# Forming the low part of the weights on GpSimd instead of VectorE in the projection stages

## The chip, the cores and the metric

The kernel runs on one core of a Trainium2 chip. A core has five engines: TensorE (PE in the profile, its weight loads PEld), VectorE (DVE), ScalarE (ACT), GpSimd (POOL) and SyncE (SP), which issues the DMAs. They run side by side and wait for each other by semaphores. The metric is the device time of one execution in microseconds; less is better.

## The reference, cut to what matters

The reference is a network of two parts in float32: two layers that mix attention, a gated recurrence, a short convolution and a Fourier branch, and then a block with latent attention, a state space scan and a feed-forward part. There are 256 context and 1024 latent positions of width 1024. What the change touches is the large projections from the normalized activations:

```python
lat = split_cols((rms_norm(h, norm_g) * (1.0 + scale) + shift) @ w_in)     # 1024 -> 3584, per layer
cx = split_cols((rms_norm(hc, norm_g) * (1.0 + scale_c) + shift_c) @ w_in)
```

and the input projection of the second block, in the same form.

## The kernel before, in words

The products need more precision than one pass of TensorE on rounded operands gives. So each operand is split in two: a high part, which is the operand rounded to the type fp32r, and a low part, which is the rest. A product is the sum of three matmuls: high by high, high by low, low by high.

`project_split` (line 358) does this for the projections. It is called nine times: three times in each of the two layers (queries, keys, values and the convolution's inputs; the Fourier branch; the recurrence's gates) and three times in the second block (latents; z; the state convolution's inputs). A call is one stage: a block of code in which each engine has its own loop over the same list of steps, with a barrier behind it. There are 384 steps in all. A step is one slice of 128 rows of the contraction (`kk`), with all the tokens and columns that are summed at that time in PSUM banks. In step i

- ScalarE (lines 465 to 478) waits until TensorE has finished step i-2, because there are NX = 2 buffers for the activations, and casts them to `x_high` (line 469). Then it casts the step's weights to `w_high` (line 473; NW = 3 buffers). Then it empties PSUM banks of a finished group, if there are any, and does a piece of work of a helper.
- VectorE (lines 497 to 511) waits for `x_high` and subtracts it from the activations, which gives `x_low` (line 500). It waits for `w_high` and subtracts it from the weights, which gives `w_low` (line 504). Then it empties banks and does its piece of the helper's work.
- TensorE (lines 515 to 536) waits for `x_low` and `w_low` and issues three matmuls for each group of the step (lines 526, 527, 528).

A helper (`beside=`) is work of another kind that is dealt out over the steps: `Heads` normalizes and rotates queries and keys, `ConvBranch` is the short convolution, `Gates` computes the recurrence's gates, `Decays` those of the state space scan, and `StateConv` (line 219) is a convolution of five taps, whose products stand at line 321. The order of everything on an engine is that of the code; nothing is planned by costs.

A step's shape is given by the width of the activations and the number of weight columns. The names in the trace are those of the tiles: `buf_a` holds the activations, `w` the weights as they came from memory, `ps` is PSUM. GpSimd has no part in these stages. Elsewhere it does sums of the softmax, parts of the recurrence (lines 862, 863) and some subtractions of the same kind as `x_low` and `w_low` (lines 3275, 3650). Line 2140 is VectorE's `x_low` in the feed-forward part, which has its own code, and line 2061 is GpSimd's product there.

Of the kernel before, what the change touches and what calls it, by code (L numbers as in the profile page):

```python
# [8 lines left out]
F32 = mybir.dt.float32  # L9
# [348 lines left out]
def project_split(k, jobs, *rooms, moves=(), beside=None, banks=8):  # L358
# [8 lines left out]
    NX, NW = 2, 3  # L367
    passes, groups, steps = [], [], []
# [37 lines left out]
    def place(name, shape):  # L406
        for room in rooms:
            if room.o + int(np.prod(shape[1:])) * 4 <= room.end:
                return room(name, shape, F32R)
        assert False, name  # L410
    xh, xl = ([place(f"x_{p}{i}", [P, width]) for i in range(NX)] for p in ("high", "low"))
    widest = max(j["cols"] for j in jobs)
    wh, wl = ([place(f"w_{p}{i}", [P, widest]) for i in range(NW)] for p in ("high", "low"))
    evac_act, evac_dve, x_high, x_low, w_high, w_low, moved, silued = sems = k.sems(
        "evacuated_by_act", "evacuated_by_dve", "x_high", "x_low", "w_high", "w_low", "moved", "silu_in_bank")
# [4 lines left out]
    def x_of(s):  # L420
        return s["job"]["x"](s["kk"], s["t0"], s["tn"])

    def w_of(s):
        return ws.tile(s["chunk"])[:, s["kk"] % KD, :]

    def evacuations(i, by):

        return [g for g in steps[i - 1]["groups"] if g["by"] == by or by == "act" and g["do"] == "times_silu"
                ] if i and steps[i - 1]["last"] else []
# [8 lines left out]
    with nc.Block() as block:  # L438
        @block.sync
        def _(sp):  # L440
            for dst, src in moves:
                sp.dma_start(dst, src).then_inc(moved, 16)
            if beside:
                beside.load(sp)
            ws.load_until(sp, ws.taken)
            if moves:
                sp.wait_ge(moved, 16 * len(moves))

        @block.scalar
        def _(act):  # L450
            def evacuate(gs):
                for i, g in enumerate(gs):
                    if i == 0 and "free" in g["job"]:
                        g["job"]["free"](act)
                    act.wait_ge(ws.products, g["ready"])
                    if g["do"] == "times_silu":
                        act.activation(g["out"], g["out"], ACT.Silu).then_inc(silued, 1)
                        continue
                    func = ACT.Silu if g["do"] == "silu" else ACT.Copy
                    dst, out = g["job"]["dst"](g["sub"], g["n"]), g["out"]  # L460
                    if len(dst.shape) == 3:
                        out = out.rearrange("p (t x) -> p t x", x=P)
                    act.activation(dst, out, func).then_inc(evac_act, 1)

            parts = beside.act(act, landed) if beside else iter(())
            for i, s in enumerate(steps):
                if i >= NX:
                    act.wait_ge(ws.products, steps[i - NX]["after"])
                act.copy(xh[i % NX][:, 0:s["tn"]], x_of(s)).then_inc(x_high, 1)  # L469
                ws.wait(act, s["chunk"])  # L470
                if i >= NW:
                    act.wait_ge(ws.products, steps[i - NW]["after"])
                act.copy(wh[i % NW][:, 0:s["job"]["cols"]], w_of(s)).then_inc(w_high, 1)
                evacuate(evacuations(i, "act"))
                if beside and i >= beside.first:
                    next(parts, None)
            evacuate(evacuations(len(steps), "act"))
            for _ in parts:
                pass

        @block.vector
        def _(dve):
            def evacuate(gs):
                for i, g in enumerate(gs):
                    if i == 0 and "free" in g["job"]:
                        g["job"]["free"](dve)
                    dve.wait_ge(ws.products, g["ready"])
                    dst = g["job"]["dst"](g["sub"], g["n"])
                    if g["onto"]:
                        if g["do"] == "times_silu":  # L490
                            dve.wait_ge(silued, g["silued"])
                        dve.wait_ge(done_of[g["onto"]["by"]], g["onto"]["count"])
                        dve.tensor_tensor(dst, g["out"], dst, ALU.mult).then_inc(evac_dve, 1)
                    else:
                        dve.tensor_copy(dst, g["out"]).then_inc(evac_dve, 1)

            parts = beside.dve(dve, landed) if beside else iter(())
            for i, s in enumerate(steps):
                dve.wait_ge(x_high, i + 1)
                dve.tensor_tensor(xl[i % NX][:, 0:s["tn"]], x_of(s), xh[i % NX][:, 0:s["tn"]].bitcast(F32),  # L500
                                  ALU.subtract).then_inc(x_low, 1)
                dve.wait_ge(w_high, i + 1)
                n = s["job"]["cols"]
                dve.tensor_tensor(wl[i % NW][:, 0:n], w_of(s), wh[i % NW][:, 0:n].bitcast(F32),  # L504
                                  ALU.subtract).then_inc(w_low, 1)
                evacuate(evacuations(i, "dve"))
                if beside and i >= beside.first:
                    next(parts, None)
            evacuate(evacuations(len(steps), "dve"))
            for _ in parts:  # L510
                pass

        @block.tensor
        def _(pe):
            parts = beside.pe(pe, landed) if beside else iter(())
            for i, s in enumerate(steps):
                pe.wait_ge(x_low, i + 1)
                pe.wait_ge(w_low, i + 1)
                for g in s["groups"]:
                    if s["kk"] == 0 and g["before"]:  # L520
                        pe.wait_ge(done_of[g["before"]["by"]], g["before"]["count"])
                    xs = [x[i % NX][:, g["a"]:g["a"] + g["tn"]] for x in (xh, xl)]
                    c = slice(g["sub"] * P, (g["sub"] + 1) * P) if s["fm"] else slice(0, s["job"]["cols"])
                    w = [v[i % NW][:, c] for v in (wh, wl)]
                    lhs, rhs = (w, xs) if s["fm"] else (xs, w)
                    pe.matmul(g["out"], lhs[0][:, :], rhs[0][:, :], start=(s["kk"] == 0), stop=False)  # L526
                    pe.matmul(g["out"], lhs[0][:, :], rhs[1][:, :], start=False, stop=False)  # L527
                    mm = pe.matmul(g["out"], lhs[1][:, :], rhs[0][:, :], start=False, stop=s["last"])  # L528
                    if s["last"]:
                        mm.then_inc(ws.products, 1)  # L530
                if not s["last"]:
                    mm.then_inc(ws.products, 1)
                if beside and i >= beside.first:
                    next(parts, None)
            for _ in parts:
                pass
# [635 lines left out]
def mixer_layer(k, layer, XT, YT):  # L1172
# [27 lines left out]
    def qkv(t, end=None):  # L1200
        r = rows[t // 5]
        return r[:, t % 5, :] if end is None else r[:, t % 5:t % 5 + end - t, :]

    heads = Heads(k, layer, qkv, qt, kt, v, spare(), KD + 1)
    project_split(k, [tm(HALF, lambda s, n: qkv(n), "copy", all_tiles),
                      fm(BR, lambda c: YT[:, 2 + c, :], "silu", ALL_BLOCKS),
                      dict(fm(HALF, lambda s: gate[:, s % 2, :], "copy", ALL_BLOCKS), second="times_silu",
# [3 lines left out]
    def unit(nk, *parts):  # L1211
# [13 lines left out]
    conv = ConvBranch(k, layer, u, gate, lay)  # L1225
    done_rows = d["branches"].rearrange("(c p) t -> p c t", p=P)
    project_split(k, [dict(fm(HALF, lambda s: fu[:, s, :] if s < 2 else YT[:, 4 + s, :], "copy", ALL_BLOCKS), silu_from=2)],
                  Layout(k, lay.o, A_C), moves=[(done_rows[:, 2:4, :], YT[:, 2:4, :])], beside=conv)
    lay = Layout(k, A_R + 2 * T * 4, A_C)
# [8 lines left out]
    rest = lay.o  # L1238
    gates = Gates(k, layer, a, key, lay, KD + 2)
    project_split(k, [fm(BR, lambda c: a[0][:, c, :], "copy", ALL_BLOCKS),  # L1240
                      fm(BR, lambda c: a[1][:, c, :], "copy", ALL_BLOCKS),
                      fm(BR, lambda c: YT[:, 4 + c, :], "silu", ALL_BLOCKS),
# [2918 lines left out]
```

## Time and profile before

| What | Value |
|---|---|
| median of 3 runs | 4411.45 us (4408.74 to 4412.24) |
| the profiled execution | 4406.21 us |
| its span | 4404.2 us |
| TensorE busy | 3866.2 us (88%) |
| TensorE's weight loads | 2991.1 us (68%) |
| VectorE busy | 2710.5 us (62%), 4101 instructions |
| ScalarE busy | 1995.1 us (45%) |
| GpSimd busy | 963.1 us (22%), 1100 instructions |

The span runs from the first to the last instruction of the profiled execution. Busy times are the union of an engine's records. Matmuls are pipelined, so that records of neighbours overlap, and 88% is not a measure of how near TensorE is to its peak. What is idle on an engine says something only if the work that ends last waits for it, so the rows further down are of single steps.

### The profile page before, as it was taken

The numbers are of one execution on the slowest core, as the hardware profiler recorded it, in microseconds if no ns is written. First come the engines' busy times: TensorE is split into PE (matmuls) and PEld (weight loads), VectorE is DVE, ScalarE is ACT, GpSimd is POOL, SyncE is SP. The second block draws the span as 40 slices with busy tenths as digits, with TensorE's granted clock in tenths as the row PEclk, the third lists the DMA queues.
The fourth block names the chain that finished last, engine by engine and source line by source line (L and its number), as shares of the span: only waits on it lengthen the run. The fifth ranks groups of instructions, "written<-read, shape, count | busy, mean of one in ns | idle before, by whom it ended". The sixth has DMA issues, their size and how long they took to land. (4 is left out here: it accounts for less than half of the span.)

```text
span 4404.2 us, 58870 instructions
## 1 busy us (share of the span) xinstructions
PE 3866.2 (88%) x22208; PEld 2991.1 (68%) x22208; DVE 2710.5 (62%) x4101; ACT 1995.1 (45%) x3667; POOL 963.1 (22%) x1100
## 2 busy tenths in 40 slices
PE   6988888987999787986789999799787979999898
PEld 5765777876775675765656666477655758888686
DVE  4756477966765567965555555447865655566555
ACT  4544265544544266434434444345543543343344
POOL 0016004610007002600055555400082000111000
PEclk7989999999999898998999999899898989999999
DMA  5100113654100111032000000212003541111243
GB/s 177 39 15 6 59 39 126 232 185 160 39 20 1 54 39 49 1 121 83 29 5 5 9 5 5 77 36 67 4 3 115 187 149 39 39 58 39 91 153 139
DMA packets 211274, 297.08 MB, mean 67 GB/s; under 512 B 74090, under 2 KB 139882, under 8 KB 210996
## 3 DMA queue, kind: packets, MB, share of 16 engines
q1 hardware_dynamic: 210436, 293.14, 20.1%
q8 instruction: 179, 2.93, 0.3%
q14 instruction: 99, 0.81, 0.1%
q0 software_dynamic: 416, 0.05, 0.0%
q10 hardware_dynamic: 144, 0.15, 0.0%
HBM read 262.17 MB, written 31.03 MB: 67 GB/s over the span
## 5 line engine op out<-in xcount | busy, mean ns | idle before, releaser
L500 DVE TENSOR_TENSOR x_low<-buf_a,x_high 128x1280 fp32r<-128x1280 f32 (+4 forms) x384 | 376.2, 980 | 430.7 <-ACT x_high L469 427.6
L526 PE MATMUL ps<-x_high,w_high 128*128 128x512 f32 (+1 forms) x1344 | 495.7, 369 | 102.8 <-DVE w_low L504 97.8
L469 ACT CAST x_high<-buf_a 128x1280 fp32r<-128x1280 f32 (+4 forms) x384 | 327.6, 853 | 560.6 <-PE ps L528 490.9
L527 PE MATMUL ps<-x_low,w_high 128*128 128x512 f32 (+1 forms) x1344 | 483.9, 360 | 0.0
L528 PE MATMUL ps<-x_high,w_low 128*128 128x512 f32 (+1 forms) x1344 | 482.9, 359 | 0.0
L2939 PE MATMUL ps<-w_high,x_high 128*128 128x512 f32 x896 | 364.6, 407 | 97.1 <-DVE w_low L2782 93.3
L526 PEld LDWEIGHTS ps<-x_high,w_high 128*128 128x128 f32 x1344 | 258.1, 192 | 174.7 <-DVE x_low L500 114.9
L2940 PE MATMUL ps<-w_low,x_high 128*128 128x512 f32 x896 | 358.7, 400 | 0.0
L2941 PE MATMUL ps<-w_high,x_low 128*128 128x512 f32 x896 | 358.5, 400 | 0.0
L2782 DVE TENSOR_TENSOR w_low<-w,w_high 128x1024 fp32r<-128x1024 f32 x170 | 208.0, 1223 | 197.8 <-ACT w_high L2895 197.7
L3469 DVE TENSOR_REDUCE mx<-ps 128x1 fp32r<-128x1280 f32 x128 | 190.7, 1491 | 199.8 <-PE ps L3344 199.3
L2895 ACT CAST w_high<-w 128x1024 fp32r<-128x1024 f32 x170 | 178.3, 1049 | 263.7 <-PE ps L2941 256.2
L2048 PE MATMUL ps<-x_high,w_high 128*128 128x512 f32 x704 | 278.1, 395 | 12.4 <-DVE w_low L2144 12.4
L528 PEld LDWEIGHTS ps<-x_high,w_low 128*128 128x128 f32 x1344 | 257.9, 192 | 38.5
L526 PE MATMUL ps<-w_high,x_high 128*128 128x512 f32 (+2 forms) x608 | 220.7, 363 | 70.1 <-DVE w_low L504 66.7
L527 PEld LDWEIGHTS ps<-x_low,w_high 128*128 128x128 f32 x1344 | 258.4, 192 | 32.6
L2050 PE MATMUL ps<-x_high,w_low 128*128 128x512 f32 x704 | 279.6, 397 | 0.0
L2049 PE MATMUL ps<-x_low,w_high 128*128 128x512 f32 x704 | 278.7, 396 | 0.0
L2939 PEld LDWEIGHTS ps<-w_high,x_high 128*128 128x128 f32 x896 | 173.6, 194 | 147.9 <-issue 111.7
L2140 DVE TENSOR_TENSOR x_low<-attn_t,x_high 128x512 fp32r<-128x512 f32 x176 | 145.5, 827 | 202.5 <-ACT x_high L2093 192.8
L2093 ACT CAST x_high<-attn_t 128x512 fp32r<-128x512 f32 x176 | 109.1, 620 | 299.2 <-PE ps L2050 297.6
L862 POOL TENSOR_TENSOR x<-a 128x128 f32<-128x128 f32 x252 | 115.9, 460 | 526.9 <-POOLq L73 421.3
(446 smaller groups left out, 8959.9 us busy)
## 6 DMA issues: line engine op xcount, KB each, us to landing
w<-in_w_out SPq DMA_DIRECT2D x26, 2048.0 KB, 8.6
w<-in_w_mod SPq DMA_DIRECT2D x24, 2048.0 KB, 9.3
w<-in_w_down SPq DMA_DIRECT2D x15, 2048.0 KB, 7.8
w<-in_w_in SPq DMA_DIRECT2D x26, 1024.0 KB, 5.2
w<-in_w_up SPq DMA_DIRECT2D x22, 1024.0 KB, 7.6
w<-in_w_in SPq DMA_DIRECT2D x7, 2048.0 KB, 9.6
x<-in_x SPq DMA_DIRECT2D x16, 512.0 KB, 8.8
scratch_branches<-buf_b SPq DMA_DIRECT2D x4, 1280.0 KB, 5.7
```

The source lines that it names most:

```text
L469: act.copy(xh[i % NX][:, 0:s["tn"]], x_of(s)).then_inc(x_high, 1)
L500: dve.tensor_tensor(xl[i % NX][:, 0:s["tn"]], x_of(s), xh[i % NX][:, 0:s["tn"]].bitcast(F32), ALU.subtract).then_inc(x_low, 1)
L526: pe.matmul(g["out"], lhs[0][:, :], rhs[0][:, :], start=(s["kk"] == 0), stop=False)
L527: pe.matmul(g["out"], lhs[0][:, :], rhs[1][:, :], start=False, stop=False)
L528: mm = pe.matmul(g["out"], lhs[1][:, :], rhs[0][:, :], start=False, stop=s["last"])
L2048: pe.matmul(o, wh[w % NW][:, c], xh[x % NX][:, :], start=(kk == 0), stop=False)
L2049: pe.matmul(o, wh[w % NW][:, c], xl[x % NX][:, :], start=False, stop=False)
L2050: mm = pe.matmul(o, wl[w % NW][:, c], xh[x % NX][:, :], start=False, stop=(kk == KD - 1))
L2782: dve.tensor_tensor(wl[i % NW][:, :], ws.tile(s["chunk"])[:, s["kk"] % PER, :], wh[i % NW][:, :].bitcast(F32), ALU.subtract).then_inc(w_lo ...
L2939: pe.matmul(o, a[:, t], wh[i % NW][:, c], start=(s["kk"] == 0), stop=False)
L2940: pe.matmul(o, a[:, t], wl[i % NW][:, c], start=False, stop=False)
L2941: mm = pe.matmul(o, b[:, t], wh[i % NW][:, c], start=False, stop=s["last"])
```

## The change

VectorE's loop in `project_split` loses the wait for `w_high` and the subtraction that forms `w_low`. A new loop of GpSimd, which had none in this function, does the same subtraction with the same operands: it waits for the step's `w_high` and for its own subtraction of the step before, and raises the same semaphore `w_low`, on which TensorE waits.

```diff
+        @block.gpsimd
+        def _(pool):
+            for i, s in enumerate(steps):
+                pool.wait_ge(w_high, i + 1)
+                if i >= 1:
+                    pool.wait_ge(w_low, i)
+                n = s["job"]["cols"]
+                pool.tensor_tensor(wl[i % NW][:, 0:n], w_of(s), wh[i % NW][:, 0:n].bitcast(F32),
+                                   ALU.subtract).then_inc(w_low, 1)
+
         @block.vector
...
                 dve.wait_ge(x_high, i + 1)
                 dve.tensor_tensor(xl[i % NX][:, 0:s["tn"]], x_of(s), xh[i % NX][:, 0:s["tn"]].bitcast(F32),
                                   ALU.subtract).then_inc(x_low, 1)
-                dve.wait_ge(w_high, i + 1)
-                n = s["job"]["cols"]
-                dve.tensor_tensor(wl[i % NW][:, 0:n], w_of(s), wh[i % NW][:, 0:n].bitcast(F32),
-                                  ALU.subtract).then_inc(w_low, 1)
                 evacuate(evacuations(i, "dve"))
```

VectorE's order in the stage with the state convolution, before; the numbers behind the names tell buffers apart:

```order
L500 TENSOR_TENSOR x_low_467_31649<-buf_a_53,x_high_465_31647 128x1280
L504 TENSOR_TENSOR w_low_472_31654<-w_2_50,w_high_469_31651 128x256
L321 SCALAR_TENSOR_TENSOR xbc_conv_461_31644<-xbc_raw_460_31643,taps_31646,xbc_conv_461_31644 128x255
L321 SCALAR_TENSOR_TENSOR xbc_conv_461_31644<-xbc_raw_460_31643,taps_31646,xbc_conv_461_31644 128x1023
L500 TENSOR_TENSOR x_low_468_31650<-buf_a_53,x_high_466_31648 128x1280
```

The same place on VectorE in the changed kernel, where line 510 is what was line 500:

```order
L510 TENSOR_TENSOR x_low_467_32001<-buf_a_53,x_high_465_31999 128x1280
L321 SCALAR_TENSOR_TENSOR xbc_conv_461_31996<-xbc_raw_460_31995,taps_31998,xbc_conv_461_31996 128x255
L321 SCALAR_TENSOR_TENSOR xbc_conv_461_31996<-xbc_raw_460_31995,taps_31998,xbc_conv_461_31996 128x1023
L510 TENSOR_TENSOR x_low_468_32002<-buf_a_53,x_high_466_32000 128x1280
L321 SCALAR_TENSOR_TENSOR xbc_conv_461_31996<-xbc_raw_460_31995,taps_31998,xbc_conv_461_31996 128x255
```

The convolution's products now stand right behind `x_low`. On GpSimd, the start of the changed program, up to the first subtractions of the first projection stage:

```order
L4155 MEMSET const-float32-0.0 128x1
L4155 MEMSET const-float32-1.0 128x1
L4155 MEMSET const-bfloat16-1.0 128x1
L4155 MEMSET const-uint8-127 128x1
L72 ISA x2
L481 UNCONDITIONAL_BRANCH
L488 ISA
L488 TENSOR_TENSOR w_low_55_725<-w_3_51,w_high_52_722 128x512
L488 TENSOR_TENSOR w_low_56_726<-w_3_51,w_high_53_723 128x512
L488 TENSOR_TENSOR w_low_57_727<-w_3_51,w_high_54_724 128x512
```

Before, the first arithmetic of GpSimd's program stood in the attention behind that stage (line 3641). Now 384 subtractions are spread over the nine stages, in the order of the steps.

## Rows read from the trace of the kernel before

**Rows 1.** The nine projection stages, sum over their windows: us busy by engine
```profile
sum 1351.00, PE 1204.53 PEld 1002.32 DVE 861.84 ACT 700.41 POOL 0.00; mean PE 133.84 PEld 111.37 DVE 95.76 ACT 77.82 POOL 0.00
```

**Rows 2.** Waits of TensorE: who waited for whom, us in total, times, longest
```profile
PEld ps L526 <- DVE x_low L500: 160.7, 88, 10.0
...
PE ps L526 <- DVE w_low L504: 164.5, 97, 30.8
```

**Rows 3.** VectorE's subtractions by form: count, us busy, mean ns, idle before, releaser
```profile
L500 DVE TENSOR_TENSOR x_low<-buf_a,x_high 128x1280 fp32r<-128x1280 f32 x128 | 190.9, 1491 | 130.3 <-ACT x_high L469 128.5
L504 DVE TENSOR_TENSOR w_low<-w,w_high 128x512 fp32r<-128x512 f32 x208 | 142.5, 685 | 24.5 <-ACT w_high L473 22.5
L500 DVE TENSOR_TENSOR x_low<-buf_a,x_high 128x640 fp32r<-128x640 f32 x96 | 79.1, 824 | 120.2 <-ACT x_high L469 119.4
L500 DVE TENSOR_TENSOR x_low<-buf_a,x_high 128x512 fp32r<-128x512 f32 x112 | 77.4, 691 | 136.3 <-ACT x_high L469 135.9
L504 DVE TENSOR_TENSOR w_low<-w,w_high 128x256 fp32r<-128x256 f32 x160 | 66.9, 418 | 0.0
```

**Rows 4.** Timeline, step of 512 columns, x 512: start and length in us
```profile
2934.49 0.69 DVE L500 TENSOR_TENSOR x_low<-buf_a,x_high 128x512 fp32r<-128x512 f32 x1 [1.43 <-ACT x_high L469]
2935.10 0.69 DVE L504 TENSOR_TENSOR w_low<-w,w_high 128x512 fp32r<-128x512 f32 x1
...
2936.35 0.39 PE L526 MATMUL ps<-w_high,x_high 128*128 128x512 f32 x1
```

**Rows 5.** Timeline, step of 256 columns, x 1280
```profile
566.94 0.40 ACT L473 CAST w_high<-w 128x256 fp32r<-128x256 f32 x1
...
567.07 1.49 DVE L500 TENSOR_TENSOR x_low<-buf_a,x_high 128x1280 fp32r<-128x1280 f32 x1 [1.67 <-ACT x_high L469]
568.48 0.42 DVE L504 TENSOR_TENSOR w_low<-w,w_high 128x256 fp32r<-128x256 f32 x1
...
569.07 0.32 PE L526 MATMUL ps<-x_high,w_high 128*128 128x256 f32 x1
```

**Rows 6.** Timeline, steps of 512 columns, x 256
```profile
242.51 0.61 ACT L473 CAST w_high<-w 128x512 fp32r<-128x512 f32 x1
...
242.57 0.36 PE L526 MATMUL ps<-x_high,w_high 128*128 128x256 f32 x1 [0.41 <-DVE w_low L504]
...
242.64 0.42 DVE L500 TENSOR_TENSOR x_low<-buf_a,x_high 128x256 fp32r<-128x256 f32 x1 [0.21 <-ACT x_high L469]
243.16 0.69 DVE L504 TENSOR_TENSOR w_low<-w,w_high 128x512 fp32r<-128x512 f32 x1
```

**Rows 7.** Timeline, step of 256 columns, x 640
```profile
688.66 0.42 DVE L504 TENSOR_TENSOR w_low<-w,w_high 128x256 fp32r<-128x256 f32 x1
...
689.22 0.36 PE L526 MATMUL ps<-w_high,x_high 128*128 128x256 f32 x1 [0.38 <-DVE w_low L504]
```

**Rows 8.** GpSimd's subtractions elsewhere, by form, columns as in rows 3
```profile
L3275 POOL TENSOR_TENSOR q_low<-q,q_high 128x512 fp32r<-128x512 f32 x16 | 20.6, 1285 | 1.3
...
L3650 POOL TENSOR_TENSOR q_low_row<-qt,q_high_twice 64x256 fp32r<-64x256 f32 x4 | 2.8, 722 | 0.2
```

**Rows 9.** Timeline of the feed-forward part, VectorE and GpSimd
```profile
3694.99 2.42 POOL L2061 TENSOR_TENSOR g_a<-g_a,act 128x1024 f32<-128x1024 f32 x1 [71.15 <-ACT act L2086]
...
3695.44 2.52 DVE L2140 TENSOR_TENSOR x_low<-attn_t,x_high 128x512 fp32r<-128x512 f32 x1 [1.38 <-ACT x_high L2093]
```

**Rows 10.** The recurrence: timeline, and line 863's ns least/median/most
```profile
709.40 0.64 DVE L945 TENSOR_TENSOR qe<-eq,qk 128x256 f32<-128x256 f32 x1
709.73 0.59 POOL L862 TENSOR_TENSOR x<-a 128x128 f32<-128x128 f32 x1
...
L863 POOL TENSOR_TENSOR x<-a x252: 392/574/669, 705.2 to 1873.5; 128x128 f32<-128x128 f32 x126
```

**Rows 11.** Timeline, a step of the gates' stage where VectorE is late
```profile
1612.22 0.40 ACT L473 CAST w_high<-w 128x256 fp32r<-128x256 f32 x1
...
1613.77 1.49 DVE L500 TENSOR_TENSOR x_low<-buf_a,x_high 128x1280 fp32r<-128x1280 f32 x1
```

## The prediction, made before the changed kernel was run

> **What bounds the kernel now.** I read the windows of the nine projection stages first: in their 1351 us TensorE has 1204.5 us of records, VectorE 861.8, and GpSimd none [rows 1]. So TensorE is near full there, and GpSimd has room in time. Then the table of waits, narrowed to TensorE: at the first matmul of a projection step its queue stands 164.5 us for VectorE's w_low and 160.7 us (by the weight load's record, partly the same time) for x_low [rows 2]. Then VectorE's instructions by form, which give the classes of the 384 steps: x_low 1280 wide in 128 steps, 640 in 96, 512 in 112, and by the code 256 in 32 and 768 in 16; w_low has 512 columns in 208 steps, 256 in 160, and 192 in the other 16 [rows 3]. Last, the timeline of one step of each class, for what is late in it.
>
> The question for a step is whether its operands are ready before TensorE has finished the step ahead. There are two x buffers, so ScalarE's cast for step i starts when step i-2 is done. From there runs a chain: x_high, x_low beside w_high, w_low, first matmul. If the chain is longer than one step of TensorE's, TensorE idles in every second step: two steps then take the chain plus one step of matmuls. So what the chain grows by, beyond its spare time, is paid once in two steps. TensorE starts 0.15 us after w_low's end at the earliest (688.66 + 0.42 = 689.08 against 689.22 [rows 7]), so spare time is what lies beyond 0.15.
>
> - 512 columns, x 512 wide: w_low ends at 2935.79 and TensorE takes the step at 2936.35 [rows 4], spare 0.41 us. The stretches with x 640 or 768 wide and 512 columns have a longer matmul part and spare over 0.8 us (my reading of their timelines; only that they have more than 0.55 matters).
> - 256 columns, x 1280 wide: w_low ends at 568.90, TensorE takes it at 569.07 [rows 5]: spare 0.02.
> - 512 columns, x 256 wide: TensorE already waits, 0.41 us at 242.57 for w_low [rows 6]. 256 columns, x 640 wide: it waits 0.38 us [rows 7]. Spare 0.
>
> **The change, part by part.** Removed from VectorE: 384 subtractions, 142.5 + 66.9 + some 5.6 us (16 of the 192 wide) = 215 us of records [rows 3]. That is a relief to an engine that has idle time in most steps, and worth something only where x_low itself starts late. Added to GpSimd: the same 384. Nothing else moves; the casts, the matmuls and the DMA queues keep their places, and GpSimd has no other work in these stages that could queue behind.
>
> Cost of one on GpSimd: the same operation, f32 minus f32 to fp32r, stands in the trace: 1.285 us for 512 columns, 0.722 us for 256 [rows 8]. VectorE takes 0.685 and 0.418 [rows 3]. For 192 columns I take 0.58, on the line through the two.
>
> The Trainium skill ("GPSIMD Engine Reference", Performance versus the Vector engine) gives 4497 ns for a tensor_tensor of 2048 columns on GpSimd, 2.2 ns a column. By that, as an estimate, 512 columns would take 1.12 us, the chain of the 512 by 512 steps would grow by 0.39 us, less than its spare, and the sum below would lose its largest class (13 us). The row for exactly this operation says 1.285, and I go by the row.
>
> When can it start? w_high ends 0.3 to 0.5 us after x_high, and VectorE is then in x_low, which reads two tensors of SBUF. The trace shows what such a pair does. VectorE's x_low of 512 columns takes 0.69 us alone [rows 3], but 2.52 us when it meets a GpSimd product that began at 3694.99 and ended at 3697.41: it ends 0.55 us after that one, so it did nothing until GpSimd had ended, but for some 0.14 us of start [rows 9]. The other way round, GpSimd's 128 column product behind VectorE's product of two SBUF tensors ends at 710.32, 0.28 us after VectorE's end at 710.04, and its record is 0.59 us against 0.39 at the least [rows 10]: it waited too, all but 0.11 us of its start. So the two run one after the other, and beside each other the change can't put them. In a steady step x_low has the way first.
>
> The growth of the chain then is, per class:
> - 512 columns, x 512 wide: x_low ends 2935.18; w_low on GpSimd ends at 2935.18 + 1.28 - 0.12 = 2936.34 instead of 2935.79, +0.55, less the spare 0.41 = 0.14. TensorE would now stand still in every second step, and a step that begins after a pause also pays some 0.1 for a pipeline that fills again (the first matmul's record is 0.36 us after a pause [rows 6, 7] and 0.32 without one, of the same 256 columns [rows 5]; 0.04 is the least, 0.1 my estimate). 56 pairs by 0.24 = 13.4 us.
> - 512 columns, x 256 wide: here x_low is over (243.06) before w_high (243.12), so nothing is in the way: 243.12 + 0.08 (the hand-off, an estimate) + 1.28 = 244.48 instead of 243.85 [rows 6], +0.63. 16 pairs: 10.1 us.
> - 256 columns, x 1280 wide: x_low ends 568.56; + 0.72 - 0.12 = 569.16 instead of 568.90, +0.26, less 0.02. 64 pairs by 0.24 = 15.4 us.
> - 256 columns, x 640 wide: +0.26, 16 pairs: 4.2 us. 192 columns: about +0.2, 8 pairs: 1.6 us.
> - x 640 or 768 wide with 512 columns, 64 steps: +0.55 is covered by the longer matmul part: 0.
> - The first step of a stage has no step ahead to hide in: six of 0.6 and three of 0.26 = 4.4 us.
> - Where VectorE is late, it gains. x_low starts at 1613.77 though x_high and w_high were done by 1612.62 [rows 11]; w_low would be formed before it, and 0.34 us of VectorE's queue goes. I count 18 such steps of 256 columns (8 have x 640 wide), nearly all in the gates' stages: -6.1. But there, and in the stage with the state convolution, GpSimd's w_low also holds up the two-tensor operations that VectorE works off beside, which gives a third back: -4 net.
>
> Sum: 13.4 + 10.1 + 15.4 + 4.2 + 1.6 + 4.4 - 4 = 45.1, say +45 us. The profiled execution took 4406.2 us (span 4404.2), 5 below the runs' median of 4411.45, so 4451 for it and 4456 on the median; I give 4454, that is 45 beyond 4409, between the two. Bounds: below, the chain grows by nothing in the 256 column classes (the case without a conflict, next part) and the filling costs nothing, +5. Above, w_low waits for one more VectorE operation in the stages with side work, +70.
>
> **Rivals.**
> 1. No conflict for the two engines: w_low begins 0.08 us after w_high. For 256 columns with x 1280 wide it ends at 567.34 + 0.80 = 568.14, before x_low (568.56), and VectorE's 0.34 us leave the chain: the step is then bound by TensorE, gain at most 0.02 in steady steps, and 0.34 in the late ones. For 512 columns nearly nothing changes, since there GpSimd hardly waits after w_high. Sum: 13.4 + 10.1 + 3.6 for the six beginnings - 6.1, less about 14 for VectorE's relief where x_low and the side work share the queue (40 steps by 0.34, an estimate), some +7: 4416. For it speaks that x_low is fully read by one engine; against it rows 9 and 10, both with f32 operands of this kind. 8%.
> 2. Faster: VectorE's queue decides. If the stages with side work (gates, state convolution, heads: some 200 steps) are held by VectorE's order, each of the 0.34 to 0.6 us taken from it counts wherever TensorE waits. Without a conflict the costs are 13.4 + 10.1 + 3.6 = 27, so it decides from 80 such steps by 0.34 on. With 110 of them, 25 steps of the 512 column classes by 0.6 beside: 27 - 37 - 15 = -25, 4384. Against it: VectorE idles 130.3 + 120.2 + 136.3 us before x_low for x_high [rows 3], so its queue is seldom what holds. 5%.
> 3. VectorE keeps the way: when x_low ends, the next operation that it has in line, a product or the state convolution's of 0.48 us, goes first, and w_low comes after it. Rows 10 speak against it (in that stretch the two alternate one by one), but there GpSimd had always been first in line. It costs one such operation, 0.3 to 1.4 us, in the 50 or so steps where a two-tensor operation stands right behind x_low and the chain is bare, mostly paid once in two steps: about +20 more, 4474. 15%.
>
> **How the numbers follow.** Forecast (one after the other, in turn) 70%, rival 1 8%, rival 2 5%, rival 3 15%; the rest, 2%, is left to something else on the faster side. Under the forecast 4454, with 4440 to 4468 from the uncertain filling (6 us) and the late steps (4 to 8 us). The range takes rival 3 in and reaches half way to rival 1: 4430 to 4480. A change under 0.2% (9 us) could not be told from none here: rival 1 lies on that edge, so faster 6%, same 8%, slower 86%.
>
> **What would show it.** After: GpSimd's w_low rows near 1.28 and 0.72 us when alone and longer where they begin inside x_low; w_low's end 0.55 (512 columns, x 512 wide) and 0.26 us (256) later against the step's x_high; PE's wait for w_low at a step's first matmul up from 164.5 us by some 40 us; new pauses in every second step of the 512 by 512 stretch near 2936, none where x is 640 wide with 512 columns. x_low should stay at 0.69 and 1.49 us in steady steps; if many of them are longer, GpSimd is first in line more often than I think. Wrong would make it: w_low rows of 256 columns that overlap x_low and still take 0.72 (rival 1), or that end only after the next VectorE operation (rival 3).

## The result, and the profile after

The changed kernel takes 4452.0 us (median of 4 runs, 4448.9 to 4452.6) against 4411.8 us before (4 runs, 4408.7 to 4413.7): a ratio of 1.0093, with a 95% interval of 1.0081 to 1.0106. It is slower by 40 us, forecast was 4454. Its profiled execution has a span of 4450.4 us, 46.2 more than before.

The sum of the windows of the nine projection stages, which answers to [rows 1], and the subtractions by form, which answer to [rows 3] (columns as there). The windows of before were cut in whole microseconds and are 9 us wider than the stages, so 1351 to 1382.5 isn't their growth: from first cast to last matmul the stages grew from 1341.8 to 1382.4, by 40.6 us.

```profile
sum 1382.50, PE 1216.80 PEld 997.54 DVE 789.64 ACT 698.51 POOL 547.62; mean PE 135.20 PEld 110.84 DVE 87.74 ACT 77.61 POOL 60.85
```

```profile
L488 POOL TENSOR_TENSOR w_low<-w,w_high 128x512 fp32r<-128x512 f32 x208 | 285.9, 1375 | 803.9 <-ACT w_high L473 802.0
L510 DVE TENSOR_TENSOR x_low<-buf_a,x_high 128x1280 fp32r<-128x1280 f32 x128 | 200.4, 1566 | 142.2 <-ACT x_high L469 140.6
L488 POOL TENSOR_TENSOR w_low<-w,w_high 128x256 fp32r<-128x256 f32 x160 | 246.0, 1538 | 447.0 <-ACT w_high L473 445.5
```

VectorE is busy 72 us less in the stages, although 215 us of subtractions left it. Part of the difference is overlap of neighbouring records, but most is waiting inside the records that stayed: added up one by one, x_low takes 29 us more than before and VectorE's other operations 84 us more. GpSimd has 548 us more: a subtraction of 256 columns has a record of 1.54 us on average, although one that runs alone takes 0.72 [rows 8], and longer than one of 512 columns. So half of such a record is waiting. x_low is longer too, 1.566 us against 1.491 [rows 3].

A steady step of 256 columns, x 1280 wide, in the timeline (start and length in us), which answers to [rows 5]:

```profile
578.00 0.40 ACT L473 CAST w_high<-w 128x256 fp32r<-128x256 f32 x1
...
578.12 1.49 DVE L510 TENSOR_TENSOR x_low<-buf_a,x_high 128x1280 fp32r<-128x1280 f32 x1 [2.33 <-ACT x_high L469]
...
578.47 1.75 POOL L488 TENSOR_TENSOR w_low<-w,w_high 128x256 fp32r<-128x256 f32 x1 [2.08 <-ACT w_high L473]
...
580.37 0.36 PE L532 MATMUL ps<-x_high,w_high 128*128 128x256 f32 x1
```

w_low begins 0.07 us after w_high and ends at 580.22, 0.61 after x_low's end at 579.61. Before, it was 0.34 after it. TensorE follows 0.15 later.

The steps of 512 columns with x 512 wide, against [rows 4], and with x 256 wide, against [rows 6]:

```profile
2972.28 0.69 DVE L510 TENSOR_TENSOR x_low<-buf_a,x_high 128x512 fp32r<-128x512 f32 x1 [2.26 <-ACT x_high L469]
...
2972.85 1.29 POOL L488 TENSOR_TENSOR w_low<-w,w_high 128x512 fp32r<-128x512 f32 x1 [1.66 <-ACT w_high L473]
...
2974.29 0.47 PE L532 MATMUL ps<-w_high,x_high 128*128 128x512 f32 x1
```

```profile
247.74 0.62 ACT L473 CAST w_high<-w 128x512 fp32r<-128x512 f32 x1
...
248.43 1.27 POOL L488 TENSOR_TENSOR w_low<-w,w_high 128x512 fp32r<-128x512 f32 x1 [1.41 <-ACT w_high L473]
...
249.85 0.36 PE L532 MATMUL ps<-x_high,w_high 128*128 128x256 f32 x1 [1.01 <-POOL w_low L488]
```

In the first, w_low is ready at 2974.14 and TensorE takes it 0.15 later: the 0.41 us that were spare are gone. In this stretch a pair of steps took 5.44 us before and takes 5.67 now, 0.23 more, where 0.24 was forecast. It doesn't show as a marked pause: the matmuls of every second step begin some 0.1 us later behind the step ahead and take some 0.1 us longer; the first has a record of 0.47 us instead of 0.39 [rows 4]. In the second, TensorE stands 1.01 us where it stood 0.41, 0.60 us more.

Cut into steps, the two traces give this. The growth is the sum of the differences from TensorE's end of one step to its end of the next; for the first step of a stage it is counted from its x_high.

| columns, x | steps | forecast, us | grown, us |
|---|---|---|---|
| 512, 512 | 111 | 13.4 | 14.5 |
| 512, 256 | 32 | 10.1 | 8.1 |
| 256, 1280 | 125 | 15.4 | 13.2 |
| 256, 640 | 32 | 4.2 | 3.0 |
| 192, 640 | 16 | 1.6 | 1.4 |
| 512, 640 or 768 | 59 | 0 | -0.4 |
| nine first steps | 9 | 4.4 | 0.8 |
| steps with VectorE late | | -4 | in the classes |
| outside the stages | | 0 | 5.6 |

The forecast's sum was 45, the spans differ by 46, the medians by 40.

The classes hold one thing more than the chain. In a few steps of either kernel TensorE's granted clock falls to its lower level, 1.2 GHz instead of 2.4, for some microseconds. Two steps of 256 columns, x 1280 wide, in the changed kernel; the last three numbers are the granted clock, the DMA share and GB/s:

```profile
3047.70:3053.10 5.40, 5.34 (x20) 4.52 (x21) 5.00 (x5) 0.01 (x1) 0.73 (x1) 0.68 0.01 3
3117.50:3121.20 3.70, 3.66 (x19) 3.08 (x20) 3.63 (x4) 0.71 (x2) 1.31 (x1) 1.00 0.00 0
```

The matmuls of the first take 5.30 us, those of the second 3.74; 0.68 is a mean, for only part of the first lies at the lower level. TensorE had stood 2.10 and 2.06 us in front of them, so what it did just before doesn't tell the two apart. Steps whose matmuls lie more than 0.6 us above their class's middle value number 9 before (14.2 us in all) and 13 after (17.8 us). Each of these has the lower level for 1.6 to 4.9 us of its length, and no other step has it for 1 us. Without that excess the growth is 14.4 us for 512 by 512, 5.5 for 512 by 256, 10.9 for 256 by 1280 and 4.4 for 256 by 640.

Of the signs that the prediction named, one failed. TensorE's wait for w_low was to go up from 164.5 us by some 40; it is 174.2. Waits for x_low come beside it in TensorE's own table, where there were 5.6 us before:

```profile
PE ps L532 <- POOL w_low L488: 174.2, 92, 31.4
...
PE ps L532 <- DVE x_low L510: 23.5, 26, 2.9
```

Together that is 28 us more. In 29 of the 384 steps w_low came first and it was x_low that was held up.

### The profile page after: what moved, and what is told of

It reads as the page before. It is cut to its first block and busy times, and to the rows that moved or that the text cites. A ratio compares the mean times of both kernels' runs of the same rounds, so it can differ in the third digit from the quotient of the medians.

```text
span 4450.4 us, 59245 instructions
## 1 busy us (share of the span) xinstructions
PE 3883.3 (87%) x22208; PEld 2991.0 (67%) x22208; DVE 2641.4 (59%) x3717; ACT 1996.5 (45%) x3667; POOL 1510.9 (34%) x1484
## 5 line engine op out<-in xcount | busy, mean ns | idle before, releaser
L488 POOL TENSOR_TENSOR w_low<-w,w_high 128x512 fp32r<-128x512 f32 (+2 forms) x384 | 547.6, 1426 | 1270.6 <-ACT w_high L473 1267.2
L510 DVE TENSOR_TENSOR x_low<-buf_a,x_high 128x1280 fp32r<-128x1280 f32 (+4 forms) x384 | 405.2, 1056 | 558.1 <-ACT x_high L469 555.2
```

The lines of the kernel that those rows point to most:

```text
L488: pool.tensor_tensor(wl[i % NW][:, 0:n], w_of(s), wh[i % NW][:, 0:n].bitcast(F32), ALU.subtract).then_inc(w_low, 1)
```

## The experiments

In the names of classes, "512 by 256" is 512 columns with x 256 wide, and the narrow classes are those of 256 and 192 columns. The theory: GpSimd's subtraction and VectorE's operations on two SBUF tensors exclude each other, w_low ends later in the chain, and the chain's growth beyond its spare time is paid once in two steps. The rivals: only the length of GpSimd's subtraction counts (no conflict), or VectorE's amount of work.

**Wide columns alone on GpSimd.**

GpSimd leaves the other steps out, and VectorE forms w_low in them as before:

```diff
+                n = s["job"]["cols"]
+                if not (n == HALF):
+                    continue
...
+                n = s["job"]["cols"]
+                if not (n == HALF):
+                    dve.wait_ge(w_high, i + 1)
+                    if i >= 1 and steps[i - 1]["job"]["cols"] != n:
+                        dve.wait_ge(w_low, i)
+                    dve.tensor_tensor(wl[i % NW][:, 0:n], w_of(s), wh[i % NW][:, 0:n].bitcast(F32),
+                                      ALU.subtract).then_inc(w_low, 1)
```

> w_low is formed on GpSimd only where the weights have 512 columns (208 steps); the steps of 256 and 192 columns stay as before. One after the other (my theory): +0.14 us and a pause in every second 512 by 512 step, +0.63 in every second 512 by 256 step, nothing where x is 640 or 768 wide: by the classes of the changed kernel's trace 14.5 + 8.1 - 0.4 = +22 us, 4434. No conflict (the rival: only GpSimd's length counts): nearly the same, +20, since w_high ends about when x_low does. So this run tells how much of the loss is GpSimd's slower subtraction alone; under 4425 both would be wrong on these classes.

Measured: 4432.5 us against 4408.5, ratio 1.0054 (1.0039 to 1.0069), +24 us. By classes: 512 by 512 +16.5, 512 by 256 +7.4, the narrow classes +1.2 in all. The rival without a conflict expected nearly the same here, so this run doesn't tell the two apart; it shows where the loss of the wide steps lies.

**Narrow columns alone on GpSimd.** The same with `n < HALF`.

> w_low is formed on GpSimd only where the weights have 256 or 192 columns (176 steps). One after the other: +13.2 + 3.0 + 1.4 = +18 us by the classes of the changed kernel's trace, 4429. No conflict: w_low would be over before x_low in the steps with x 1280 wide and the chain shorter by 0.34 us, so no loss, and a gain of some 10 to 20 where VectorE is late: 4392 to 4410.

Measured: 4422.2 us against 4408.5, ratio 1.0032 (1.0019 to 1.0045), +14 us, where the rival without a conflict had no loss or a gain. The two halves add up to 38 us of the 40 to 44 by which the changed kernel is slower. So the loss is, as far as these runs can tell, the sum over the steps and not one effect of GpSimd's presence. The class 256 by 1280 grows by 7.5 us here and by 13.2 in the changed kernel. The steps at the lower clock make the difference: without them it is 11.3 and 10.9.

**Each subtraction on GpSimd done twice.** A single execution. `once` is a semaphore of its own, declared with the others.

```diff
...
                 n = s["job"]["cols"]
+                pool.tensor_tensor(wl[i % NW][:, 0:n], w_of(s), wh[i % NW][:, 0:n].bitcast(F32),
+                                   ALU.subtract).then_inc(once, 1)
+                pool.wait_ge(once, i + 1)
                 pool.tensor_tensor(wl[i % NW][:, 0:n], w_of(s), wh[i % NW][:, 0:n].bitcast(F32),
                                    ALU.subtract).then_inc(w_low, 1)
```

> The changed kernel with each of the 384 subtractions on GpSimd done twice, one after the other's end. The chain grows by another 1.3 us for 512 columns and 0.75 for 256. If growth beyond the spare time is paid once in two steps: 56 pairs by 1.3 (512 by 512) = 73, 16 by 1.3 (512 by 256) = 21, 24 pairs of 512 by 640 by 0.55 + 1.3 - 0.86 = 24, 8 of 512 by 768 by 0.4 = 3, 80 pairs of 256 columns by 0.75 = 60, less where VectorE is late, 8 of 192 by 0.6 = 5: +186 over the changed kernel, 4638. If it were paid in each step: near +370, 4820. If GpSimd were off the chain: no change.

Measured: 4680.6 us, 229 more than the changed kernel, against 186 for payment once in two steps and 370 for each step. The class that tells most is 512 by 640, which had lost nothing in the changed kernel (45 steps): it grows by 24.3 us, forecast 24. The missing 43 us are in the first steps (21 us more, which I had forgotten), in 512 by 768 (9.0 instead of 3), and for some 13 us in steps at the lower clock, of which this kernel has more (21, with 30.8 us of excess, against 13 with 17.8). Without those, the classes 512 by 512, 512 by 256 and the two of 256 columns grow by 75, 20 and 60 us over the changed kernel, where 73, 21 and 60 were expected. So the count by pairs is borne out. Two steps of the 512 by 512 stretch in this kernel:

```profile
3173.94 1.29 POOL L488 TENSOR_TENSOR w_low<-w,w_high 128x512 fp32r<-128x512 f32 x1 [1.31 <-ACT w_high L473]
3175.30 1.27 POOL L491 TENSOR_TENSOR w_low<-w,w_high 128x512 fp32r<-128x512 f32 x1
...
3176.72 0.47 PE L535 MATMUL ps<-w_high,x_high 128*128 128x512 f32 x1 [0.98 <-POOL w_low L491]
...
3179.80 0.47 PE L535 MATMUL ps<-w_high,x_high 128*128 128x512 f32 x1
```

The pause of 0.98 us stands in front of one step, and the next, 3.08 us later, follows with none marked (0.1 us by the records). That isn't so everywhere. Some 25 us earlier in the same stretch each step has its pause:

```profile
3151.24 0.47 PE L535 MATMUL ps<-w_high,x_high 128*128 128x512 f32 x1 [0.53 <-POOL w_low L491]
...
3154.75 0.47 PE L535 MATMUL ps<-w_high,x_high 128*128 128x512 f32 x1 [0.53 <-POOL w_low L491]
```

Of the 111 steps of the class 95 have a pause over 0.1 us. What is fixed is the sum of two steps, 7.0 us in both places against 5.67 in the changed kernel: two steps take the chain plus one step of matmuls, however the pause is dealt out between them.

**x_low by an operation that reads one tensor, first on the kernel before, then on the changed one.** Both leave out the subtraction of x_high, so that their results aren't the reference's.

```diff
-                dve.tensor_tensor(xl[i % NX][:, 0:s["tn"]], x_of(s), xh[i % NX][:, 0:s["tn"]].bitcast(F32),
-                                  ALU.subtract).then_inc(x_low, 1)
+                with nc.allow_low_precision(reason="low part"):
+                    dve.tensor_reduce(xl[i % NX][:, 0:s["tn"]], x_of(s).unsqueeze(2), AX.X, ALU.add).then_inc(x_low, 1)
```

> The kernel before with x_low made by an operation that reads one tensor instead of two (a sum over groups of one element of x, which leaves out the subtraction of x_high; x_low is then x). w_low stays on VectorE. If that operation takes as long as the subtraction (0.69 us for 512, 1.49 for 1280) the time is that of before, 4412; its rows tell. It is the base for the next kernel.

> The changed kernel with the same x_low, which reads one tensor (it leaves out the subtraction of x_high), so that VectorE's x_low does not ask for what GpSimd reads through. To be compared with the kernel before with that x_low. If two-tensor operations and GpSimd's exclude each other: w_low no longer waits for x_low, w_low rows take 0.72 us in steady steps of 256 columns, the steps with x 1280 wide lose nothing, and what is left is 512 columns (+20) less VectorE's relief: +5 to +15 over its base. If GpSimd waited for something else, the loss is the same 40 us over its base.

Measured: the base 4408.3 us (ratio to the kernel before 0.9998, 0.9988 to 1.0008), and with w_low on GpSimd 4406.7 us (0.9997, 0.9988 to 1.0006). The loss of 40 us is gone, by a change of x_low's operation alone. A step of the stretch that was shown first for the changed kernel (256 columns, x 1280 wide):

```profile
571.27 1.49 DVE L511 TENSOR_REDUCE x_low<-buf_a 128x1280 fp32r<-128x1280 f32 x1 [1.97 <-ACT x_high L469]
...
571.62 0.74 POOL L488 TENSOR_TENSOR w_low<-w,w_high 128x256 fp32r<-128x256 f32 x1 [2.71 <-ACT w_high L473]
...
573.23 0.28 PE L532 MATMUL ps<-x_high,w_high 128*128 128x256 f32 x1
```

VectorE's operation is as long as before, 1.49 us, GpSimd's begins as early after x_low's start, and it takes 0.74 instead of 1.75 us. So it is x_low's subtraction that w_low waits for in the changed kernel. The sum differs from it in what it reads and also in kind, and these two runs don't separate that. By classes, against the kernel before: 256 by 1280 -17.7 us, 256 by 640 -1.1, 192 by 640 -1.6, but 512 by 512 +12.9 and 512 by 256 +6.5. So in the narrow classes the conflict was all of the loss and hid a gain; in the wide ones GpSimd's length is nearly all of it. I had expected +5 to +15 over the base and it is -1.6: the gain of the narrow classes, 20 us, was taken too small. Whether it comes from less work on VectorE or from a chain without w_low in it, the next experiment tells.

**The weights one step ahead, w_low on VectorE.** The chain holds w_low only because it is formed for the step at hand. With three weight buffers it can be formed for the next one. On VectorE it stands behind x_low of step i.

```diff
+            def cast_weights(j):
+                if j >= len(steps):
+                    return
+                ws.wait(act, steps[j]["chunk"])
+                if j >= NW:
+                    act.wait_ge(ws.products, steps[j - NW]["after"])
+                act.copy(wh[j % NW][:, 0:steps[j]["job"]["cols"]], w_of(steps[j])).then_inc(w_high, 1)
...
                 act.copy(xh[i % NX][:, 0:s["tn"]], x_of(s)).then_inc(x_high, 1)
-                ws.wait(act, s["chunk"])
-                if i >= NW:
-                    act.wait_ge(ws.products, steps[i - NW]["after"])
-                act.copy(wh[i % NW][:, 0:s["job"]["cols"]], w_of(s)).then_inc(w_high, 1)
+                if i == 0:
+                    cast_weights(0)
+                cast_weights(i + 1)
...
-                dve.wait_ge(w_high, i + 1)
-                n = s["job"]["cols"]
-                dve.tensor_tensor(wl[i % NW][:, 0:n], w_of(s), wh[i % NW][:, 0:n].bitcast(F32),
-                                  ALU.subtract).then_inc(w_low, 1)
+                for j in ([0, 1] if i == 0 else [i + 1]):
+                    if j < len(steps):
+                        n = steps[j]["job"]["cols"]
+                        dve.wait_ge(w_high, j + 1)
+                        dve.tensor_tensor(wl[j % NW][:, 0:n], w_of(steps[j]), wh[j % NW][:, 0:n].bitcast(F32),
+                                          ALU.subtract).then_inc(w_low, 1)
```

> All on VectorE as before, but ScalarE casts the weights of step i+1 behind x_high of step i, and VectorE subtracts them behind x_low of step i, so that w_low is out of the chain from TensorE's end of step i-2 to its start of step i (three weight buffers are there). If the chain sets the time, the pauses in every second step of the narrow classes go: 8 pairs by 0.36 (192 columns), 16 by 0.4 (256 by 640), 16 by 0.4 (512 by 256) = 16 us, and some 5 to 15 in the steps with side work where w_low is late: 4411.8 - 20 to - 30, about 4387. If VectorE's amount of work sets it there, only the 16 us come: 4396.

Measured: 4378.3 us against 4408.5, ratio 0.9929 (0.9914 to 0.9944): 30 us faster than the kernel before, 74 faster than the changed one, and 9 below the expected 4387. The narrow classes gain 19.7 us, as much as in the one-tensor kernel (20.4), though no work left VectorE. So that gain needs no relief of VectorE; a chain without w_low in it is enough. The step of 512 columns, x 256 wide:

```profile
234.55 0.69 DVE L513 TENSOR_TENSOR w_low<-w,w_high 128x512 fp32r<-128x512 f32 x1
235.47 0.43 DVE L507 TENSOR_TENSOR x_low<-buf_a,x_high 128x256 fp32r<-128x256 f32 x1 [0.23 <-ACT x_high L477]
...
236.27 0.28 PE L535 MATMUL ps<-x_high,w_high 128*128 128x256 f32 x1
```

w_low is ready 0.23 us before x_low starts, and the first matmul has no pause in front. Both kernels of the comparison are beaten.

**The weights one step ahead, w_low on GpSimd.** The same order of casts, in the changed kernel.

> The changed kernel with the weights one step ahead: ScalarE casts those of step i+1 behind x_high of step i, and GpSimd subtracts them. The chain no longer holds w_low, so the loss of 40 us must go if it came from the chain. One after the other: in the stages without side work as fast as with VectorE one step ahead; in those with side work VectorE loses 0.34 us of queue and gets 0.6 us (256 columns) or 1.2 us (512) of standing behind GpSimd whenever a two-tensor operation follows: within 5 us of the VectorE version, 4390. No conflict: VectorE's relief is a clear gain, 15 to 20 us better than the VectorE version, 4370.

Measured: 4400.4 us, ratio 0.9981 (0.9971 to 0.9991). The loss of the changed kernel is gone, as expected, but this one lies 22 us behind the VectorE version, where I had expected the two within 5. x_low and the first product of the heads' side work, on VectorE, in the GpSimd version and then in the VectorE version:

```profile
L517 DVE TENSOR_TENSOR x_low<-buf_a,x_high 128x1280 fp32r<-128x1280 f32 x128 | 204.2, 1595 | 129.9 <-ACT x_high L477 128.3
...
L766 DVE TENSOR_TENSOR qkv<-qkv,stat 128x384 f32<-128x384 f32 x20 | 19.2, 960 | 0.1
```

```profile
L507 DVE TENSOR_TENSOR x_low<-buf_a,x_high 128x1280 fp32r<-128x1280 f32 x128 | 190.8, 1490 | 119.3 <-ACT x_high L477 117.8
...
L762 DVE TENSOR_TENSOR qkv<-qkv,stat 128x384 f32<-128x384 f32 x20 | 11.0, 552 | 0.1
```

**The same with x_low by the operation that reads one tensor.**

> The kernel with the weights one step ahead and w_low on GpSimd, with x_low made by the operation that reads one tensor (it leaves out the subtraction of x_high). It tells why the GpSimd version (4400) lies 22 us behind the VectorE version (4378). In it x_low no longer excludes GpSimd's work, VectorE's side work still does (qkv, t, turning, xbc_conv, a, e with two tensors). If GpSimd, started late because x_low goes first, then stands in front of the side work and that is the loss: with w_low running beside x_low it is over before the side work starts, and the 22 us and VectorE's relief come back: 4360 to 4375. If the side work would meet w_low in any case: 4390 to 4400. If the loss has nothing to do with what is read: 4400.

Measured: 4376.0 us, ratio 0.9921 (0.9905 to 0.9938). The 22 us are regained when x_low reads one tensor, and the product of the heads falls from 0.96 to 0.77 us. So the GpSimd version lost by what x_low and w_low do to each other. Two things went together here. In the GpSimd version x_low's records are some 35 us longer in all than in the VectorE version, and those of VectorE's other work in the stages 76 us longer. Now x_low's are as short as ever and the others still 47 us longer. Which of the two cost the 22 us, the run doesn't separate. It is no faster than the VectorE version, 4378.3: the medians lie 2 us apart, less than the two runs can tell apart. So taking 215 us of work from VectorE brought nothing that can be measured here, net of the conflict with the side work that remains.

## Why the prediction was right

*The chain and its spare time.* The timelines gave a step-by-step price, and the classes came out within 2.2 us each, the nine first steps excepted. The mechanism, payment once in two steps, held when the cost was doubled. The closeness of the sum is luck in part. Without the steps at the lower clock, 512 by 256 and 256 by 1280 grew by 5.5 and 10.9 us where 10.1 and 15.4 were forecast, both too dear by 4.5. And the median grew by 40, not 45.

*GpSimd's length.* 1.285 us was forecast for 512 columns, 1.27 is measured alone. For 256, 0.722 and 0.74. By the figure of the Trainium skill that the prediction weighed ("GPSIMD Engine Reference", Performance versus the Vector engine), as an estimate 1.12 us for 512 columns, the 512 by 512 steps would have lost nothing. They lost 14.5 us, and the row was the right guide.

*One after the other.* w_low's end +0.61 us after x_low's for 256 columns, where 0.60 was forecast. The experiment with a one-tensor x_low settles rival 1: it is the kernel without that conflict, and it lies 1.6 us under its base, where rival 1's sum had 7 above.

*The six and three first steps.* TensorE's start of a stage's first step came 0.52 to 0.55 us (six stages) and 0.24 to 0.25 us (three) later, near the 0.6 and 0.26 of the forecast. But the matmuls of the first steps run in part at the lower clock (granted 0.62 in the first stage's first step before, 0.71 after) and took from 1.1 us less to 0.1 more than before, so that the table shows 0.8 for 4.4.

*VectorE late.* This term was mis-sized in its parts. The row that stood for it [rows 11] has this counterpart:

```profile
1642.89 1.48 DVE L3062 SCALAR_TENSOR_TENSOR e<-e 128x1280 f32<-128x1280 f32 x1
1644.41 1.92 DVE L510 TENSOR_TENSOR x_low<-buf_a,x_high 128x1280 fp32r<-128x1280 f32 x1
...
1643.29 1.69 POOL L488 TENSOR_TENSOR w_low<-w,w_high 128x256 fp32r<-128x256 f32 x1 [2.53 <-ACT w_high L473]
```

w_low waited for VectorE's side work, ended 0.61 us after it, and held up x_low, which took 1.92 instead of 1.49 us. Both operands are there 1.96 us after the side work's end. Before, that was 1.86: the side work ended at 1613.74 and w_low at 1615.60. So the step that was to gain 0.34 us lost 0.1. What such a step would gain from VectorE's relief alone no run shows, for the narrow classes gain as much where nothing was taken from VectorE.

*Rival 2*, faster by VectorE's relief, did not come; in the last experiment, with w_low out of the chain, VectorE's relief shows no gain beyond what the runs can tell apart.

*Rival 3*, that VectorE's next operation goes ahead of w_low, did not happen. A step of the state convolution's stage, with a two-tensor product right behind x_low:

```profile
3065.57 1.49 DVE L510 TENSOR_TENSOR x_low<-buf_a,x_high 128x1280 fp32r<-128x1280 f32 x1
3065.85 1.81 POOL L488 TENSOR_TENSOR w_low<-w,w_high 128x256 fp32r<-128x256 f32 x1 [1.96 <-ACT w_high L473]
3066.98 2.28 DVE L321 SCALAR_TENSOR_TENSOR xbc_conv<-xbc_raw,taps,xbc_conv 128x255 f32<-128x255 f32 x2
```

w_low ends 0.60 us after x_low, as where nothing stands behind it. I count 76 steps in which w_low began inside x_low and an operation with two tensors stood right behind it; w_low ends 0.58 to 0.61 us (256 columns) or 1.12 to 1.16 us (512) after x_low in every one.

*What stays open.* 5.6 us of the growth lie outside the nine stages, 2.7 of them in the attention behind the first. No experiment was made on them. They may be the spread from one execution to another: the profiled execution of the kernel with the one-tensor x_low on VectorE, whose median is that of before, has 3.5 us more outside the stages too.

## What to carry to other kernels

An idle engine isn't a free one: before work is moved from VectorE to GpSimd, look in the trace for a pair of theirs that overlaps and reads two SBUF tensors on VectorE, and price the move as if the two ran in turn, for VectorE's operations too: here they grew by 113 us for 215 taken away. Price it on the chain of one step, with its spare time and the number of buffers, not by busy shares. And where an operand can be formed a step early, its place in the order is worth more (30 us here) than the engine that forms it.

## What was not expected of the hardware

A sum over groups of one element (tensor_reduce, 128x1280 from SBUF) took the same 1.49 us as the subtraction of two tensors, and GpSimd ran beside it undisturbed: 0.74 us for 256 columns. In the GpSimd version with the weights ahead, also VectorE operations with a scalar and one tensor in SBUF (a of the gates, 128x1280, eight of them) went from 0.82 us before to 1.23 on average, so two tensors as input aren't the only thing that meets GpSimd.
